# Start-up loads of the modulation spread over own buffers, a third bank for convolved chunks, moved squares, side loads and reduction, in a four-layer mixed-attention kernel

## The reference

```python
def first_block(x, c, positions, w_ada, b_ada, norm_mix, w_in, dn_conv, ...):
    c_act = jax.nn.silu(c)
    for l in range(DEPTH):
        mod = c_act @ w_ada[l] + b_ada[l]
        sh1, sc1, gt1, sh2, sc2, gt2 = [m[:, None, :] for m in jnp.split(mod, 6, axis=-1)]
        h = rms_norm(x, norm_mix[l]) * (1.0 + sc1) + sh1
        proj = h @ w_in[l]
        dn_qkv, dn_z, dn_a, dn_b, sw_q, sw_k, sw_v, gate_a, gate_b = _split_columns(proj, IN_SIZES)
        dn_qkv = jax.nn.silu(causal_dwconv(dn_qkv, dn_conv[l]))
        ...
        y_a = o_dn.reshape(B, T, DN_WIDTH) @ w_dn_out[l]
        ...
        y_b = swa_sink_attention(sq, sk, sv, swa_sinks[l]) @ w_swa_out[l]
        merged = jax.nn.sigmoid(gate_a) * y_a + jax.nn.sigmoid(gate_b) * y_b
        x = x + gt1 * (merged @ w_o[l])
        h = rms_norm(x, norm_ffn[l]) * (1.0 + sc2) + sh2
        up_act, up_lin = jnp.split(h @ w_up[l], 2, axis=-1)
        up_act = causal_dwconv(up_act, ffn_conv[l]) + ffn_conv_b[l]
        x = x + gt2 * ((jax.nn.silu(up_act) * up_lin) @ w_down[l])
    return x
```

## Time and profile before

| | |
|---|---|
| median of 3 runs | 2565.71 us |
| lowest, highest | 2561.35, 2568.26 us |
| profiled execution, its own time | 2560.55 us |
| its span | 2558.8 us |
| PE busy | 2306.8 us (90%) |
| DVE, ACT, POOL busy | 1568.0, 1053.4, 529.9 us |
| DMA | 384.25 MB, mean 150 GB/s |

### The profile page before, as it was taken

How to read it: one execution, slowest core, us unless ns; L and a number is a source line. 1 busy time by engine, 2 the same in 40 slices (tenths; PEclk the granted TensorE clock), 3 DMA queues, 4 the chain that set the end, 5 groups by cost and what they waited for, 6 DMA issues and landing times.

```text
span 2558.8 us, 41650 instructions
## 1 busy us (share of the span) xinstructions
PE 2306.8 (90%) x18185; PEld 2214.9 (87%) x18185; DVE 1568.0 (61%) x1892; ACT 1053.4 (41%) x1294; POOL 529.9 (21%) x286
## 2 busy tenths in 40 slices
PE   1789898889998998898899999996999999977999
PEld 0787898889998878888799999985999999977999
DVE  4673456656766635666566655678555655686554
ACT  1344115533334442164343543454433533545433
POOL 2442320636834323207340000000000000000000
PEclk9899799989999988999999999997999999988999
DMA  7463003655765630045465555542455555532554
GB/s 229 150 210 99 17 1 100 194 185 198 251 218 159 214 99 1 1 127 186 159 208 179 177 185 182 178 135 66 148 182 182 181 182 182 165 99 77 187 182 132
DMA packets 332575, 384.25 MB, mean 150 GB/s; under 512 B 12391, under 2 KB 315114, under 8 KB 332266
## 3 DMA queue, kind: packets, MB, share of 16 engines
q1 hardware_dynamic: 332394, 381.59, 46.5%
HBM read 380.51 MB, written 1.05 MB: 149 GB/s over the span
## 4 chain that ended last, share of the span: by engine, by line
PE 42%; DVE 6%; ACT 2%; issue 0%; ACTq 0%; DVEq 0%
PE bank L646 9%; PE bank L647 9%; PE bank L648 9%; PE bank L835 4%; PE bank L836 4%; PE bank L837 4%; DVE weights_low L1174 2%; ACT weights_high L1814 1%; DVE arena L1271 1%; ACT h_high L1836 0%; PE bank L663 0%; PE bank L665 0%; PE bank L664 0%; DVE small L1697 0%; ACT arena L1837 0%
## 5 line engine op out<-in xcount | busy, mean ns | idle before, releaser
L1174 DVE TENSOR_TENSOR weights_low<-ring,weights_high 128x2048 fp32r<-128x2048 f32 x310 | 754.5, 2434 | 506.9 <-ACT weights_high L1814 506.8
L646 PE MATMUL bank<-h_high,weights_high 128*128 128x256 f32 x3424 | 984.8, 288 | 55.7 <-DVE arena L1271 23.2
L647 PE MATMUL bank<-h_low,weights_high 128*128 128x256 f32 x3424 | 967.2, 282 | 0.0
L648 PE MATMUL bank<-h_high,weights_low 128*128 128x256 f32 x3424 | 966.5, 282 | 0.0
L1814 ACT ACTIVATE weights_high<-ring 128x2048 fp32r<-128x2048 f32 x310 | 593.2, 1914 | 779.1 <-PE bank L648 549.9
L646 PEld LDWEIGHTS bank<-h_high,weights_high 128*128 128x128 f32 x3424 | 650.5, 190 | 76.1 <-issue 43.2
L647 PEld LDWEIGHTS bank<-h_low,weights_high 128*128 128x128 f32 x3424 | 651.7, 190 | 3.1 <-issue 2.9
L648 PEld LDWEIGHTS bank<-h_high,weights_low 128*128 128x128 f32 x3424 | 651.0, 190 | 0.0
L835 PE MATMUL bank<-hidden_high,weights_high 128*128 128x256 f32 x1056 | 299.7, 284 | 0.9 <-DVE hidden_low L1408 0.8
L836 PE MATMUL bank<-hidden_low,weights_high 128*128 128x256 f32 x1056 | 299.1, 283 | 0.0
L837 PE MATMUL bank<-hidden_high,weights_low 128*128 128x256 f32 x1056 | 299.1, 283 | 0.0
(11 more groups left out here) (388 smaller groups left out, 3088.4 us busy)
## 6 DMA issues: line engine op xcount, KB each, us to landing
ring<-in_w_in SPq DMA_DIRECT2D x80, 1024.0 KB, 5.2
ring<-in_w_up SPq DMA_DIRECT2D x44, 1024.0 KB, 5.2
ring<-in_ffn_w_gate SPq DMA_DIRECT2D x44, 1024.0 KB, 5.4
ring<-in_ffn_w_up SPq DMA_DIRECT2D x44, 1024.0 KB, 5.4
ring<-in_ffn_w_down SPq DMA_DIRECT2D x44, 1024.0 KB, 4.9
side<-in_w_ada SPq DMA_DIRECT2D x42, 1024.0 KB, 7.8
...
```

What stands on the lines that cost most here:

```text
L646: mm(o[:, m, :], a_, high[:, t, :], start=(t == 0), stop=False)
L647: mm(o[:, m, :], a_, low[:, t, :], start=False, stop=False)
L648: last = mm(o[:, m, :], b_, high[:, t, :], start=False, stop=(t == KT - 1))
L1174: v.tensor_tensor(low, wide(q), high.bitcast(F32), ALU.subtract).then_inc(chunk_split, 1)
```

## The change

1. **Start.** Four of the eight modulation chunks of layer 0's first two groups (`ADA_V` is now 4, 6, 7, 0) get buffers of their own in the arena (`start_at`), each with its semaphore, and stay with DVE's `modulate`. The other four (ring chunks 5 and 1, side chunks 2 and 3) are weighed by PE alone, `weigh_start`: 16 matmuls of one column straight from the float32 weights. POOL's first two sums are gone. Only the 256 constant columns needed at once and 8 more are loaded first; the other 2688 columns are loaded behind qkv chunk 0 (`k_landed`). x is loaded fourth, and PE transposes it without waiting for the rows. The small rows are issued partly by ACT (20), partly by SP (27) in groups between the big loads. The angles of the rotary embedding are computed behind the low half of qkv chunk 0 on DVE, their sine and cosine on ACT inside the first qkv step.
2. **Banks.** The 12 qkv chunks of each layer turn over three banks (`PLACE`, `PREV`), the third is `B[3]`.
3. **Side loads.** Of the four behind dno 1, two stay and two now stand behind wo 1 and wo 3. The reduction of group 4 (`mod_reduce(l, 4)`) moves from behind wo 1 to behind the last square sum after wo 3.
4. **Squares.** In layers of the first block ACT squares pair i - 1 before it rounds the chunk after wo i; only the last pair is left to `norm`. On DVE the scaling stands before the low half of ul 0, not after.
5. **Feed-forward start.** For i = 0 DVE convolves ua 0 before it makes the low half of ua 1.

The core of the diff; what only follows from it (semaphores, moved lists of the same rows) is left out:

```diff
-ADA_V = (4, 5, 6, 7, 0, 1)
-ADR_AFTER = {("swq", 2): 2, ("swq", 3): 3, ("wo", 1): 4}
+ADA_V = (4, 6, 7, 0)
+ADA_PE = (5, 1)
+ACT_LOADS = 20
+ADR_AFTER = {("swq", 2): 2, ("swq", 3): 3, ("wo", 3): 4}
...
+        for start, steps in (("qkv", 0), even(18, 6)), (("ga", 2), [0, 0]), (("dno", 1), [0, 1, 8, 10]), (("ua", 0), even(28, 12) if l == 0 else even(10, 4)):
...
-        posf, ta, tb_, tc_ = (ar(8192 + 256 * i, T) for i in range(4))
+        posf, ta, tb_, tc_ = (gab[:, i, :] for i in range(4))
+        start_at = [ar(at, KT, T) for at in (6144, 8192, 10240, 12288)]
...
+        PLACE, PREV, last_in = {}, {}, {}
+        for key in R:
+            at = key[2] % 3 if key[0] == "qkv" else R[key] % 2
+            PLACE[key] = (LV + [B[3][:, :].rearrange("p (m t) -> p m t", m=2)])[at]
+            PREV[key] = last_in.get(at)
+            last_in[at] = key
...
-                if R[key] >= 2:
-                    pe.wait_ge(*release(by_turn[R[key] - 2]))
-                o = LV[R[key] % 2]
+                if PREV[key] is not None:
+                    pe.wait_ge(*release(PREV[key]))
+                o = PLACE[key]
...
+            load_start(0)
+            load_chunk(0)
+            load_rows(ACT_LOADS, ACT_LOADS + 5)
+            load_start(1)
+            load_rows(ACT_LOADS + 5, ACT_LOADS + 10)
             load_side(0)
+            load_rows(ACT_LOADS + 10, ACT_LOADS + 15)
+            load_start(2)
+            load_rows(ACT_LOADS + 15, ACT_LOADS + 20)
             load_side(1)
...
+            load_rows(ACT_LOADS + 20, N_IN)
+            load_start(3)
+            load_chunk(1)
+            load_chunk(2)
             for q in range(NS, len(chunks)):
                 load_chunk(q)
+                if q == NS:
+                    sp.dma_start(K[:, 2 * P:C_COL], a["shape_constants"][:, 2 * P:C_COL]).then_inc(k_landed, 16)
...
+            def weigh_start(c, w, used):
+
+                r = R["adr", 0, c // 4]
+                for m in range(2):
+                    at = 2 * (c % 4) + m
+                    for t in range(KT):
+                        last = mm(L[r % 2][:, at:at + 1], w[:, t, m * P:(m + 1) * P], ccol[:, t:t + 1], start=(t == 0), stop=(t == KT - 1))
+                last.then_inc(used, 1)
...
                     linear3(("wo", l, i), h_high, h_low, ready=(merge_split, 4 * l) if i == 0 else None)
-                    if i == 1:
-                        mod_reduce(l, 4)
                     if i >= 2:
                         sum_pair(2 * l + 1, i - 2)
                 sum_pair(2 * l + 1, 2)
                 sum_pair(2 * l + 1, 3)
+                mod_reduce(l, 4)
...
-                    if i == 1:
-                        modulation(l, 4)
+                modulation(l, 4)
+                scale(2 * l + 1, lambda t: scol[:, 8 + t:9 + t], 24)
                 split(SI["ua", l, 0] + 2)
-                scale(2 * l + 1, lambda t: scol[:, 8 + t:9 + t], 24)
                 vf = VT[2, l]
                 for i in range(FP):
-                    split(SI["ul", l, i] + 2)
+                    if i:
+                        split(SI["ul", l, i] + 2)
...
-                    if i:
-                        split(SI["ul", l, i] + 3)
+                    split(SI["ul", l, i] + (3 if i else 2))
...
                 if l == 0:
-                    split(SI["s1", l, 0] + 2)
-                norm(2 * l, 0, SI["s1", l, 0] + 2)
+                    norm(0, 0, 0, SI["s1", 0, 0] + 1)
+                    split(SI["s1", 0, 0] + 2)
+                    act.wait_ge(start_v, 2)
+                    a_(nea[:, :], heads[:, R_ALOG:R_ALOG + 16], ACT.Exp).then_inc(start_a, 1)
...
                 for i in range(4):
+                    if i:
+                        norm_squares(2 * l + 1, i - 1)
                     split(SI["wo", l, i] + 2)
-                norm(2 * l + 1, 24, SI["ua", l, 0] + 2)
+                norm(2 * l + 1, 24, SI["ua", l, 0] + 2, made_squares=3)
```

226 lines of the change are left out of this document (129 added, 97 removed).

## The result

The changed kernel takes 2500.71 us (median of four runs, 2494.76 to 2504.20) beside 2565.52 us for the kernel before in the same session: a ratio of 0.9751, 95% interval 0.9736 to 0.9765. The forecast was 2468 us with a range of 2454 to 2490. So the sign was right and the size was not: 65 us gained where 97 were forecast.

What follows compares the result with a forecast made beforehand. PE, busy 2306.8 of 2558.8 us, was taken to bound all but the first 95 us; terms 44 + 18.6 + 17 + 13 + 3.8 = 96.4 us off the 2565.7 us median gave 2469, rounded to 2468 us, range 2454 to 2490.

Steps and rivals of the forecast that it cites:

- B: qkv chunks: with three banks, 14 of PE's waits for the convolution go, -18.6 us.
- C: swo, both layers: side loads placed further on no longer delay the swo weight chunks, -17 us.
- E: Feed-forward start: convolving ahead of the next low half removes most of the third chunk's waits, -3.8 us.
- A: Start: only bytes hold the loads, so qkv chunk 0 starts at about 50.5 us, not 95.42; -44 us.
- Rival 1: Start: small row issues stay uncovered, x or the wide chunk lands late; A is 31, 2481 us; chance 0.13.
- D: wo to feed-forward start: squares between roundings and reduction behind wo 3 shorten the stretch, -13 us over both layers.
- Rival 2: wo and qkv: DVE and POOL collide at their port; B 14, C 14, D 8, 2481 us; chance 0.12.
- rivals 3 and 4: 3: qkv's third bank does little, B 4, 2483 us, chance 0.07; 4: lower granted clock makes the kernel slower, 0.03.

Runs made afterwards that it cites:

- half-weighing run: Changed kernel, but PE weighs only row tiles 0 to 3 of eight in each of its four start modulation chunks (result incomplete): 2493.98 us.
- the kernel with POOL clear of the norm: Changed kernel with the third side load of group 4 one place later and the feed-forward's side loads four chunks later: 2481.35 us.

## Why the prediction was wrong

**The sum's frame held.** B, C and E were worked out as waits that go and what is late next. B: 18.6 us forecast, 18.0 us in the landmarks, 18.5 us of waits back with two banks. C: 17 us forecast, 17.2 us measured. E: 3.8 us forecast; counted from ua 0 the third feed-forward chunk came 3.0 us sooner in layer 0 and 1.6 us in layer 1, and the rows of the table gave 2.8 us and some part of 2.5 us. That the low half is late next, "inside 5.8 us", held in qkv too (no wait over 1.1 us).

**A, 44 us forecast, 30.7 measured: the step that failed is "PE weighs the other four chunks, 16 row blocks at one column each (1.84 us for a like 16)".** The row is 16 records of eight matmuls, each float32 matmul leaving two; and it stands at full clock. A chunk is 16 matmuls, 32 records, and PE ran them near half clock: 6.96, 9.13 for two and 6.99 us, 23.1 us in all where the term, four times 1.84, had 7.4, and then 3.55 us of reduction. Of the 15.7 us too few, 7.3 are the row misread (four times 32 records at full clock are 14.7 us), the other 8.4 the clock. The prediction placed that work between landings; it was a chain without a gap from 20.94 to 48.3 us. I had said that the modulation would be done at 38.3 us; it was at 48.9. In the half-weighing run it was at 42.4, and since POOL had not begun by then, the first matmul followed 1.7 us later: that makes the 10.9 us. The rest, 6.1 us from the first scaling to the first matmul where 1.9 was allowed, is POOL's first sum: the prediction has no word on it, though its side load stands behind that of qkv chunk 0 as before and moved forward with it (issued at 36.67 us, not 56.42). So the first qkv chunk came 14.2 us after the 50.5 us of the forecast: 10.6 us by the modulation, 4.2 by POOL, 0.9 by the wide matmuls, less 1.5 us that the forecast had allowed behind them. Landing was late too (37.75 for 33.3 us; the first 10 us moved 243 GB/s, not 328), hidden behind PE. Rival 1 (rows uncovered, A 31) gives nearly the measured A by luck and is wrong all the same: from 10 to 40 us the loads ran at 341 GB/s and more.

**D, 13 us forecast, -5.8 measured: the step that failed is "A low half beside POOL took 3.98 us, not 2.29, so up to 1.8 us for each of two chunks; I take 1.6 us a layer, 3.2 us in all".** The gain before that deduction was put at 8.6 and 7.6 us; with POOL out of the way of the scaling it is 8.2 and 6.3 us (40.31 and 39.38 down to 32.1 and 33.1), and layer 1 still has 1.7 us of the collision in wo 0. So the mechanism and its size stand. What was mis-sized is the collision: 3.2 us forecast, 20.3 measured (14.5 won, 5.8 lost). I priced it for the weights' low halves alone, which have slack, and these cost 0.94 us. It fell on three short operations at which PE already stands: the two low halves of the merge, 0.68 us each become 2.83 and 1.76, and after them the half clock; the scaling, 0.47 become over 2; and the first low half of h, 1.48 us. What blocks is the length of POOL's operation, not that of DVE's own.

The Trainium skill ("SBUF — State Buffer", section "SBUF: two separate sides") has it so: of VectorE with two SBUF inputs and GpSimd, the one that starts first keeps the pair of ports for its whole instruction and the other waits. The trace agrees, at 2.1 us and more for an operation of 0.47 us, which ends 0.28 us after POOL's, and at the two orders of start in wo 0 above. The rule was in the prediction, applied to low halves; there it gave D "about 8 us" (its own figures, 2.5 us for each of two chunks in two layers off 16.2 us, make it 6), and it was not asked which DVE operation is next in the chain when a whole sum comes by. That the trace "bears the lock out but not the full price" was a reading of one place. At the start of the same trace of the kernel before, a low half takes 2.1 us more than its 2.29, nearly a whole operation of POOL's (2.38), and two scalings take 2.34 us instead of 0.9:

```profile
79.37 4.43 DVE L1174 TENSOR_TENSOR weights_low<-ring,weights_high 128x2048 fp32r<-128x2048 f32 x1
83.72 2.34 DVE L1208 SCALAR_TENSOR_TENSOR arena<-x,scol,rinv 128x256 f32<-128x256 f32 x2
```

Rival 2 named the cause and was priced 14 us too low at D (8 us for -5.8), while its losses at B and C did not come. Nor did the sign that the prediction gave for it, low halves of weights of 3.5 us and more with PE waiting: the longest in wo was 3.16 us, and PE's one wait for one 0.94 us.

**The rivals 3 and 4 did not come:** the third bank gives all it was to give, and the mean clock is 0.957, after 0.960. But the clock takes part in another way. In seven kernels whose start is the same in code the first wide matmul came between 55.0 and 58.1 us, and the half-clock stretches before it fell in different places; and most of 7 us won at the start was gone at 428 us. That the clock's stretches are the cause is my reading, not shown by a run. A sum of waits can't see it.

**What stays open:** why the granted clock stays low while PE is busy with one-column matmuls, and whether another placing of layer 0's DVE-bound stretch would keep the start's gain. Neither was tried. Nor was a placing in which no sum of POOL's stands near the merge's low halves: the kernel with POOL clear of the norm still loses 1.7 us in layer 1 to it.
